# A one-core decoder layer: normalization squares summed on VectorE, router and last shared tile on column groups, and the experts' table written in two parts

## The chip, the cores and the metric

The kernel runs on one core of one Trainium2 chip. The metric is the device time of one execution in microseconds (us). Every view of the trace is of one profiled execution.

## The reference, cut to what matters

One decoder layer over 520 rows of 1024 channels (512 prompt rows and 8 sample rows). Three sub-layers, each followed by a layer norm of `ALPHA * x + f(x)`:

```python
def layer_norm(x, g, b):
    mu = jnp.mean(xf, axis=-1, keepdims=True)
    var = jnp.mean(jnp.square(xf - mu), axis=-1, keepdims=True)
    return (xf - mu) * lax.rsqrt(var + LN_EPS) * g + b

def decoder_layer(...):
    mix = jnp.concatenate([y_a, y_b], axis=-1) @ p['w_out']      # RG-LRU group and convolution group
    x = layer_norm(ALPHA * x + mix, ln1_g, ln1_b)
    x = layer_norm(ALPHA * x + cross_attn(x, mem_k, mem_v, w_q, w_o), ln2_g, ln2_b)
    x = layer_norm(ALPHA * x + moe(x, ...), ln3_g, ln3_b)

def moe(x, ...):
    scores = jax.nn.sigmoid(x @ w_router)            # 64 experts
    # the best 4 of 8 groups, the best 8 experts in them; gates = scores / their sum * 2.5
    return swiglu(x, w1_s, w3_s, w2_s) + routed_experts(x, idx, gates, w1_e, w3_e, w2_e)
```

Each expert is a SwiGLU of 1024 to 256 to 1024 channels, with 3 MB of weights.

## The kernel before, in words

The engines' programs are written out by hand, one block for each (`sync` SP, `gpsimd` POOL, `tensor` PE, `scalar` ACT, `vector` DVE), and meet at semaphores. The PSUM memory is four buffers of 128 x 1024, handed out in the order of a list of groups (`GROUPS`): group g waits until group g-4 has been taken out (`open_group`, `emptied`). `wait_full` waits until PE has finished a group, `wait_out` until it was taken out. An fp32 matmul is two records in the trace.

**Start.** SP loads the five tiles of x, then `w_in` in eight slabs. POOL issues five parameter loads, clears `ident`, issues four state loads and completes the identity (L559). PE turns the tiles of x with it (`turn`, L765), then runs the first projection slab by slab (`mm`, L750); after the seventh slab it turns the parameters.

**First norm.** x lies as `xT`, eight chunks of 128 channels x 520 rows. The mean is one group of matmuls against `mean_d` (all 1/1024). DVE subtracts it from the eight chunks (L1781), ACT squares each (L1406) into `sq`, and `norm_var("var1")` sums the eight squares in PSUM with 8 x 2 matmuls of 260 columns, each waiting for its square on `s_sq`. PE has `v1a` ahead of it and `v1b` and the q projection behind it. ACT takes the root, DVE the reciprocal and the scaling, ACT the gain.

**Second norm**, by halves of 260 rows. `half_var("var2a", 0)` stands in PE's order inside the sample attention's output group `os` (8 samples; it comes before the sixth), with the copies of `os`, its transposes and the second half's projection `xb` behind it. `half_var("var2b", 1)` stands between the shared expert's `h3a0` and `h1b0`; then the router follows, `rt0` and `rt1` (8 matmuls of 64 weight columns x 260 moving columns each; `rt1` waits for each chunk's gain, L1498). On DVE, `half_center` (L1903) is followed by `half_scale`, in the second half with `gated("h3a0", 0)` (L1922) between them. ACT takes `h1b0` with a Silu, then both router groups with a Sigmoid (L1525), PE turns the scores (`rtT`) after tile `x20` of x, and DVE starts the choice of the experts (L1954).

**Routing.** DVE computes the choice, PE sorts the experts by load (`key`, `beaten`, `swT`, `sorted`, `order`) and counts each row's place in its expert (`rank`, `count`). From the order DVE writes `table` (L2027 to L2034, all 64 experts and five tiles at once: the gate in three bf16 parts, and the number among the row's choices by a scan, L2032), then the places (L2037, L2039), the largest count (L2041 to L2044) and `s_table`.

**Head of the experts' stage.** PE does `shared_out(0)` (2 x 2 matmuls of 512 columns from the shared expert's hidden values), waits for `s_table`, and then

```python
            a_step(0, 0)
            a_step(1, 1)
            shared_out(1)
            a_step(2, 2)
            shared_out(2)
            a_step(3, 3)
            shared_out(3)
            shared_out(4)
            wait_out(pe, "so4")
            b_step(0, 0, 16)
            c_step(0, 0, 48)
```

`a_step` finds an expert's rows (five bf16 matmuls of 6 columns of a one-hot from DVE, `oh_step` L2059, against `table`). DVE turns the result into indices (`i_step`, L2065 to L2070), POOL gathers the rows (L660), `b_step` turns them, ACT copies (L1550), `c_step` is the up projection, `t_step` and `y_step` turn the hidden values and project down. `shared_sum(t)` (L2054) on DVE adds shared tile t to `base`. Tile 4 has 8 rows. Of each eight experts five are heavy (112 rows in the first eight, 96 later) and three are light (64 rows). A light expert's up projection (`up_few`) alternates between output partitions 0 to 63 and 64 to 127.

**Experts.** 64 of them in a software pipeline. The weights have four slots; SP issues expert e+4 when `y_step(e)` is done (L495 to L497). Each gather is issued by POOL some steps ahead. At the end the rows written by the experts are loaded again, summed and normalized.

## Time and profile before

| | us |
|---|---|
| median of 3 runs | 1221.01 |
| lowest and highest | 1220.01, 1221.20 |
| the profiled execution's own time | 1218.57 |
| its span, first to last instruction | 1216.8 |
| PE busy in the span | 1138.4 (94%) |
| DVE busy | 411.7 (34%) |
| ACT busy | 257.2 (21%) |
| POOL busy | 176.1 (14%) |

The busy share of PE says which engine most of the time is spent behind, not that each matmul is needed where it stands. The chain of waits names what released each piece. A timeline row gives start and length in us, the engine and line, the operation with its shape, the count that was merged, and in brackets the idle time before it with what ended it. The mean granted TensorE clock of the span is 0.978 of 2.4 GHz.

### The profile page before, as it was taken

How to read it: one execution, taken by the hardware profiler on the slowest of the kernel's cores; microseconds unless marked ns; L12 is line 12 of the kernel's file. 1: busy time of each engine (PE TensorE's matmuls, PEld its weight loads, DVE VectorE, ACT ScalarE, POOL GpSimd, SP SyncE). 2: the span in 40 equal slices, each digit the busy share in tenths (PEclk: the TensorE clock that was granted, in tenths of full speed). 3: DMA queues.
4: the chain of work that ended last, by engine and by line, in shares of the span. 5: the costliest groups of instructions: out<-in, count | busy, mean ns of one | idle time of the engine just before them, and what ended most of it. 6: DMA issues, size and time to landing. Idle time of an engine off the chain costs nothing.

```text
span 1216.8 us, 21054 instructions
## 1 busy us (share of the span) xinstructions
PE 1138.4 (94%) x8302; PEld 759.3 (62%) x8302; DVE 411.7 (34%) x1016; ACT 257.2 (21%) x564; POOL 176.1 (14%) x210
## 2 busy tenths in 40 slices
PE   7999997999988999889999999999999999999964
PEld 6888645877865788657755555555655555655410
DVE  0369997122048324821121212122121121111133
ACT  1101334022041125101122222122222222222200
POOL 3120050000000000111122222122221222212100
PEclk9999998999999999999999999999999999999978
DMA  9630404034047353346999999999999999999496
GB/s 332 235 139 1 156 13 173 1 138 156 1 140 258 157 209 156 155 143 243 352 384 384 385 389 384 380 386 388 388 388 380 371 381 393 384 389 385 161 367 269
DMA packets 66313, 319.16 MB, mean 262 GB/s; under 512 B 10311, under 2 KB 16671, under 8 KB 39629
## 3 DMA queue, kind: packets, MB, share of 16 engines
q1 hardware_dynamic: 51269, 278.60, 59.9%
q0 software_dynamic: 13568, 35.48, 8.6%
q10 hardware_dynamic: 1424, 4.35, 0.9%
q8 instruction: 37, 0.61, 0.2%
q14 instruction: 15, 0.12, 0.0%
HBM read 300.15 MB, written 29.36 MB: 271 GB/s over the span
## 4 chain that ended last, share of the span: by engine, by line
PE 72%; DVE 14%; DMA 10%; issue 1%; ACT 1%; SPq 1%; POOL 0%; POOLq 0%; DVEq 0%
PE psum L750 65%; DVE act_mem L1704 7%; PE psum L765 7%; DMA arena<-in_w_e_dram 5%; DMA arena<-y_rows 3%; DVE mk_mem L1863 2%; DMA arena<-in_w_in_dram 1%; DMA act_mem<-x_rows,idx_x 1%; SPq L541 0%; DVE act_mem L1801 0%; DVE act_mem L1718 0%; DVE rstd L1792 0%; DVE act_mem L1799 0%; DVE act_mem L1769 0%; DMA y_rows<-act_mem,idx_y 0%
## 5 line engine op out<-in xcount | busy, mean ns | idle before, releaser
L750 PE MATMUL psum<-arena,act_mem 128*32 128x128 f32 (+6 forms) x4800 | 512.3, 363 | 6.0 <-DMA arena<-in_w_e_dram 5.1
L750 PEld LDWEIGHTS psum<-arena,act_mem 128*32 128x32 f32 (+5 forms) x4800 | 263.4, 124 | 193.8 <-issue 110.7
L750 PE MATMUL psum<-act_mem,arena 128*128 128x260 f32 (+1 forms) x1728 | 352.4, 366 | 6.0 <-ACT act_mem L1550 2.0
L750 PEld LDWEIGHTS psum<-act_mem,arena 128*128 128x128 f32 x1728 | 306.0, 192 | 49.7 <-ACT act_mem L1550 2.4
L765 PE MATMUL psum<-ident,act_mem 96*128 96x96 f32 (+8 forms) x484 | 76.8, 288 | 19.3 <-POOL ident L559 6.8
L673 POOL DMA_INDIRECT y_rows<-act_mem,idx_y x40 | 45.1, 1128 | 320.2 <-DVE idx_x L2080 170.5
L2092 DVE TENSOR_SCALAR act_mem<-psum,act_mem 96x512 f32<-96x512 f32 (+1 forms) x40 | 29.9, 748 | 155.6 <-PE psum L750 155.6
L1704 DVE SCALAR_TENSOR_TENSOR act_mem<-act_mem,wcb 128x511 f32<-128x511 f32 (+29 forms) x120 | 77.7, 728 | 0.0
L765 PEld LDWEIGHTS psum<-ident,act_mem 96*128 96x128 f32 (+8 forms) x484 | 56.5, 174 | 32.3 <-issue 8.6
L2089 DVE TENSOR_TENSOR act_mem<-act_mem,psum 128x192 f32<-128x192 f32 x35 | 12.4, 354 | 175.5 <-ACT act_mem L1560 175.5
L750 PEld LDWEIGHTS psum<-act_mem 128*96 128x96 bf16 (+4 forms) x371 | 28.5, 126 | 57.2 <-issue 51.2
L1560 ACT ACTIVATE act_mem<-psum 128x192 f32<-128x192 f32 x35 | 11.6, 330 | 189.1 <-PE psum L750 189.1
L1574 ACT ACTIVATE act_mem<-psum,act_mem 96x512 f32<-96x512 f32 (+1 forms) x40 | 27.3, 683 | 111.3 <-PE psum L750 111.3
L666 POOL DMA_INDIRECT y_rows<-act_mem,idx_y x24 | 24.3, 1012 | 162.2 <-DVE idx_x L2070 152.2
L750 PE MATMUL psum<-act_mem 128*96 (+7 forms) x371 | 42.8, 234 | 4.9 <-DVE act_mem L2059 4.9
L765 PEld LDWEIGHTS psum<-ident,mk_mem 64*128 64x128 f32 (+7 forms) x316 | 36.7, 190 | 15.7 <-issue 13.0
L765 PE MATMUL psum<-ident,mk_mem 64*128 64x64 f32 (+7 forms) x316 | 42.4, 276 | 4.3 <-DVE mk_mem L1863 2.6
L750 PE MATMUL psum<-arena,sum_rows 128*32 128x512 f32 (+1 forms) x132 | 23.5, 761 | 21.0 <-DMA arena<-y_rows 21.0
L750 PE MATMUL psum<-arena,kv_mem 128*128 128x512 f32 x96 | 41.8, 593 | 1.2 <-ACT kv_mem L1378 1.2
L1555 ACT ACTIVATE act_mem<-psum 128x384 f32<-128x384 f32 x70 | 30.5, 488 | 24.8 <-PE psum L765 24.8
L660 POOL DMA_INDIRECT act_mem<-x_rows,idx_x x32 | 31.2, 976 | 18.8 <-issue 9.5
L1352 ACT ACTIVATE act_mem<-psum,par 128x520 f32<-128x520 f32 x24 | 16.1, 695 | 81.8 <-PE psum L750 81.7
(264 smaller groups left out, 729.2 us busy)
## 6 DMA issues: line engine op xcount, KB each, us to landing
arena<-in_w_e_dram SPq DMA_DIRECT2D x192, 1024.0 KB
arena<-y_rows SPq DMA_DIRECT2D x8, 2048.0 KB, 23.5
arena<-in_w_in_dram SPq DMA_DIRECT2D x16, 512.0 KB, 18.3
arena<-in_cache_mem_k_dram SPq DMA_DIRECT2D x8, 1024.0 KB, 9.0
arena<-in_cache_mem_v_dram SPq DMA_DIRECT2D x8, 1024.0 KB, 11.8
arena<-in_w_v_dram SPq DMA_DIRECT2D x1, 4096.0 KB, 24.5
arena<-in_w_k_dram SPq DMA_DIRECT2D x1, 4096.0 KB, 13.9
arena<-in_w_out_dram SPq DMA_DIRECT2D x1, 4096.0 KB, 13.9
```

Of the source, the lines that this page charges most:

```text
L660: gp.indirect_dma_start(out=xg[b][0:cap, :], out_offset=None, in_=x2_rows[:, :], in_offset=bass.IndirectOffsetOnAxis(ap=idx_x[0:cap, n:n + ...
L666: gp.indirect_dma_start(out=y_rows[:, :].rearrange("r (h n) -> (r h) n", h=2), out_offset=bass.IndirectOffsetOnAxis(ap=idx_y[:, n:n + 1], ...
L673: gp.indirect_dma_start(out=y_rows[:, :], out_offset=bass.IndirectOffsetOnAxis(ap=idx_y[0:cap, n:n + 1], axis=0), in_=ys[0:cap, b, :], in_ ...
L750: return pe.matmul(out, lhsT, rhs, start=first, stop=last)
L765: return pe.transpose(out, in_, ident[0:n, 0:n])
L1352: act.activation(out, two(bank(name)), func, **kw).then_inc(s_emA, 1)
L1555: last = act.activation(xgT[:, b, 4 * h:4 * h + 4, 0:MCAP], psum[:, 1, 512 * h:512 * h + 4 * MCAP].rearrange("p (k s) -> p k s", k=4), ACT ...
L1574: return act.activation(ys[0:cap, b, 0:512], psum[0:cap, 0, 0:512], ACT.Copy, scale=picked[0:cap, n, 1:2])
L1704: return dve.scalar_tensor_tensor(out, in0, w, in1, ALU.mult, ALU.add)
L1863: ins = dve.tensor_tensor_reduce(junk, kc[:, m, XD * h:XD * h + XD], q_all[:, b, XD * h:XD * h + XD], 1.0, 0.0, ALU.mult, ALU.add, ss[:, m ...
L2089: return dve.tensor_tensor(silu[:, b, 0:192], silu[:, b, 0:192], psum[:, 2, 512 * b + 192:512 * b + 384], ALU.mult)
L2092: return dve.tensor_scalar(ys[0:cap, b, 512:1024], psum[0:cap, 0, 512:1024], picked[0:cap, n, 1:2], None, ALU.mult)
```

## The change

1. **Identity first.** On POOL the clearing of `ident` and its completion stand ahead of the parameter and state loads.
2. **var1.** DVE adds the squares in four pairs (`s_pair`), and PE sums four of them, 4 x 2 matmuls in place of 8 x 2.
3. **var2a, var2b.** DVE adds all eight squares of a half into `xsum` (seven additions, each waiting for the one before, `s_sqsum`), and PE does one matmul of 260 columns in place of eight. In the second half these additions stand ahead of `gated("h3a0", 0)`.
4. **Router.** Each matmul of 260 columns becomes two of 130, to output partitions 0 to 63 and 64 to 127; ACT takes each half with a Sigmoid of its own.
5. **Shared tile 4.** Four column groups of 32 partitions with 256 columns each, 16 records on PE in place of 8 of 512 columns; DVE adds it in four instructions.
6. **Table in two parts.** Columns of the first four experts first, then the places and `oh_step(0)`, `oh_step(1)`; the count after these; the other 60 experts' columns between the shared sums, and `s_table` after them. The subtraction of 1 from the places is gone (POOL numbers the slots from 1). PE no longer waits for `s_table`; its waits for PSUM are put before each user, and `b_step(0)` waits for `so2`, `c_step(0)` for `so3`.

```diff
@@ POOL
+            gp.memset(ident[:, :], 0.0).then_inc(s_const, 1)
+            gp.wait_ge(s_const, 1)
+            gp.affine_select(out=ident[:, :], ...).then_inc(s_const, 1)
             load_parameters(gp, PAR_SPEC[8:], s_par2)
-            gp.memset(ident[:, :], 0.0).then_inc(s_const, 1)
             gp.dma_start(st_h, I["state_rglru_h"][0]).then_inc(s_state, 16)
...
-            gp.wait_ge(s_const, 1)
-            gp.affine_select(out=ident[:, :], ...).then_inc(s_const, 1)
@@ PE
-            norm_var("var1", mean_d, sq, KC)
+            wide("var1", lambda k: mean_d[:, :], lambda k: sq[:, k, :], range(0, KC, 2),
+                 before=lambda k: pe.wait_ge(s_pair, k // 2 + 1))
+            norm_at[0] += KC
...
             def half_var(name, h):
-                half_wide(name, lambda k: mean_d[:, :], lambda k: sq[:, k, :], range(KC), h,
-                          before=lambda k: pe.wait_ge(s_sq, norm_at[0] + k + 1))
-                norm_at[0] += KC
+                pe.wait_ge(s_sqsum, h + 1)
+                half_wide(name, lambda k: mean_d[:, :], lambda k: xsum[:, 0, :], range(1), h)
...
-                    last = mm(ps[0:E, 0:HALF], wr[:, k, :], xT[:, k, HALF * h:HALF * h + HALF], k == 0, k == KC - 1)
+                    for q in range(2):
+                        at = HALF * h + QUARTER * q
+                        last = mm(ps[E * q:E * q + E, 0:QUARTER], wr[:, k, :], xT[:, k, at:at + QUARTER], k == 0, k == KC - 1)
...
+                            for q in (2 * n, 2 * n + 1):
+                                last = mm(ps[32 * q:32 * q + w, 0:256], shT[:, k, t * P:t * P + w],
+                                          w2s[:, k, 256 * q:256 * q + 256], k == 0, k == 1)
...
+            wait_out(pe, "order")
             shared_out(0)
-            pe.wait_ge(s_table, 1)
-            wait_out(pe, "count")
-            wait_out(pe, "x24")
...
+            wait_out(pe, "x24")
             a_step(0, 0)
             a_step(1, 1)
+            wait_out(pe, "rank")
             shared_out(1)
             a_step(2, 2)
+            wait_out(pe, "count")
             shared_out(2)
             a_step(3, 3)
+            wait_out(pe, "so0")
             shared_out(3)
+            wait_out(pe, "so1")
             shared_out(4)
-            wait_out(pe, "so4")
+            wait_out(pe, "so2")
             b_step(0, 0, 16)
+            wait_out(pe, "so3")
             c_step(0, 0, 48)
             b_step(1, 1, 16)
+            wait_out(pe, "so4")
@@ DVE
+            for k in range(0, KC, 2):
+                dve.wait_ge(s_sq, RC + k + 2)
+                dve.tensor_tensor(sq[:, k, :], sq[:, k, :], sq[:, k + 1, :], ALU.add).then_inc(s_pair, 1)
             norm_scale("var1", xT, KC)
...
+            def half_square_sum(h):
+                at = RC + KC + KC * h
+                dve.wait_ge(s_sq, at + 2)
+                total = half(xsum[:, 0, :], h)
+                ins = dve.tensor_tensor(total, half(sq[:, 0, :], h), half(sq[:, 1, :], h), ALU.add)
+                for k in range(2, KC):
+                    link(ins)
+                    dve.wait_ge(s_sq, at + k + 1)
+                    ins = dve.tensor_tensor(total, total, half(sq[:, k, :], h), ALU.add)
+                ins.then_inc(s_sqsum, 1)
...
             half_center("mean2b", 1)
+            half_square_sum(1)
             gated("h3a0", 0)
...
+            def shares(at):
+                sh, tab = share_p[:, :, at], table[:, :, at]
+                link(dve.tensor_copy(tab[:, :, :, 3], sh))
+                link(dve.tensor_tensor(sh, sh, tab[:, :, :, 3], ALU.subtract))
+                link(dve.tensor_copy(tab[:, :, :, 4], sh))
+                link(dve.tensor_tensor(tab[:, :, :, 5], sh, tab[:, :, :, 4], ALU.subtract))
+
+            def turns(last, at):
+                for t in range(TT):
+                    n = chain(dve.tensor_tensor_scan(left[:, t, 0:last], wsum[:, 0:last], sel_p[:, t, 0:last], 0.0,
+                                                     ALU.mult, ALU.add))
+                dve.wait_ge(s_v, n)
+                link(dve.tensor_scalar(table[:, :, at, 2], left[:, :, at], 1.0, None, ALU.subtract))
+
+            shares(slice(0, FIRST))
+            turns(FIRST, slice(0, FIRST))
             wait_full(dve, "rank")
...
             oh_step(0, 0)
             oh_step(1, 1)
+            wait_full(dve, "count")
+            link(dve.tensor_tensor(counts, bank("count")[:, 0:E], bump, ALU.add))
+            dve.tensor_reduce(cmax, counts, AX.X, ALU.max).then_inc(s_emV, 1)
+            wait_out(dve, "count")
+            dve.tensor_copy(over[:, :], cmax).then_inc(s_over, 1)
             i_step(0, 0, None)
             oh_step(2, 2)
             i_step(1, 1, None)
             oh_step(3, 3)
             shared_sum(0)
+            shares(slice(FIRST, E))
             shared_sum(1)
+            turns(E, slice(FIRST, E))
+            dve.sem_inc(s_table, 1)
             i_step(2, 2, None)
             oh_step(4, 4)
             shared_sum(2)
```

## Rows read from the trace of the kernel before

**Rows 1.** The page's chain that ended last, by engine.

```profile
PE 72%; DVE 14%; DMA 10%; issue 1%; ACT 1%; SPq 1%; POOL 0%; POOLq 0%; DVEq 0%
```

**Rows 2.** Timeline of PE, 0 to 36 us.

```profile
6.85 5.92 PE L765 MATMUL psum<-ident,act_mem 128*128 128x128 f32 x40 [6.85 <-POOL ident L559]
...
22.53 10.79 PE L750 MATMUL psum<-act_mem,arena 128*128 128x260 f32 x48 [0.59 <-DMA arena<-in_w_in_dram]
```

**Rows 3.** Timeline of all engines, 255 to 365 us: the first norm.

```profile
263.16 4.94 DVE L1781 TENSOR_TENSOR act_mem<-act_mem,psum 128x520 f32<-128x520 f32 x8 [1.25 <-PE psum L750]
...
269.82 7.18 PE L750 MATMUL psum<-act_mem,mean_d 128*128 128x260 f32 x32
```

**Rows 4.** Timeline of all engines, 385 to 478 us: the second norm, first half.

```profile
413.55 0.43 DVE L1893 TENSOR_TENSOR act_mem<-act_mem 128x260 f32<-128x260 f32 x1
...
414.78 2.77 DVE L1903 TENSOR_TENSOR act_mem<-act_mem,psum 128x260 f32<-128x260 f32 x8 [0.80 <-PE psum L750]
...
419.10 3.77 PE L750 MATMUL psum<-act_mem,mean_d 128*128 128x260 f32 x16
```

**Rows 5.** The same timeline: the second half and the router.

```profile
460.55 2.77 DVE L1903 TENSOR_TENSOR act_mem<-act_mem,psum 128x260 f32<-128x260 f32 x8 [2.98 <-PE psum L750]
...
463.86 3.67 PE L750 MATMUL psum<-act_mem,mean_d 128*128 128x260 f32 x16
...
467.56 0.48 ACT L1493 ACTIVATE rstd<-psum,eps_t 128x260 f32<-128x260 f32 x1 [2.43 <-PE psum L750]
...
470.96 7.23 PE L750 MATMUL psum<-act_mem,gate_w 128*64 128x260 f32 x32
```

**Rows 6.** Timeline of all engines, 478 to 590 us and just before: the scores.

```profile
477.44 0.38 ACT L1525 ACTIVATE kv_mem<-psum 64x260 f32<-64x260 f32 x1
...
478.23 0.38 ACT L1525 ACTIVATE kv_mem<-psum 64x260 f32<-64x260 f32 x1 [0.41 <-PE psum L750]
...
479.14 0.51 PE L765 MATMUL psum<-ident,kv_mem 64*128 64x64 f32 x5
```

**Rows 7.** Timeline of PE, 535 to 600 us: a light expert's up projection.

```profile
557.02 3.85 PE L750 MATMUL psum<-arena,act_mem 128*64 128x256 f32 x32
```

**Rows 8.** Timeline of all engines, 478 to 590 us: DVE's work for the table and the first experts.

```profile
505.00 1.86 DVE L2027 CAST act_mem<-kv_mem 128x320 bf16<-128x320 f32 x1
...
510.59 0.70 DVE L2034 TENSOR_SCALAR act_mem<-kv_mem 128x320 bf16<-128x320 f32 x1
...
512.72 1.40 DVE L2059 TENSOR_TENSOR act_mem<-act_mem,gate_w 128x560 bf16<-128x560 f32 x2
...
514.24 0.16 DVE L2065 TENSOR_REDUCE act_mem<-psum 112x2 f32<-112x6 f32 x1
...
516.53 1.21 DVE L2054 SCALAR_TENSOR_TENSOR act_mem<-act_mem,psum 128x1024 f32<-128x1024 f32 x1
```

**Rows 9.** The same timeline and its continuation: PE in that stretch.

```profile
505.00 3.67 PE L750 MATMUL psum<-act_mem 128*128 128x512 f32 x8
...
513.61 17.71 PE L750 MATMUL psum<-act_mem 128*112 128x6 bf16 x52 [4.93 <-DVE act_mem L2059]
...
534.77 7.79 PE L750 MATMUL psum<-act_mem,arena 128*128 128x112 f32 x64 [1.01 <-ACT act_mem L1550]
```

**Rows 10.** The chain of waits: a gather from issue to landing.

```profile
676.75 10.88 DMA act_mem<-x_rows,idx_x
```

**Rows 11.** Windows: us, busy of PE, PEld, DVE, ACT, POOL, granted clock, DMA share, GB/s.

```profile
388.50:391.20 2.70, 0.14 (x2) 0.10 (x2) 2.49 (x13) 0.00 (x0) 0.00 (x0) 1.00 1.08 405
...
512.00:518.80 6.80, 5.19 (x15) 2.86 (x16) 5.41 (x15) 0.00 (x0) 2.83 (x3) 0.50 1.01 427
...
771.30:774.80 3.50, 3.50 (x20) 2.00 (x18) 0.00 (x0) 0.00 (x0) 0.94 (x1) 0.51 1.00 414
...
822.00:860.00 38.00, 38.00 (x368) 22.12 (x366) 8.12 (x24) 8.47 (x23) 10.21 (x10) 1.00 1.02 385
```

**Rows 12.** Timeline of PE, 766 to 776 us: a wait for an expert's weights.

```profile
770.76 5.44 PE L750 MATMUL psum<-arena,act_mem 128*64 128x256 f32 x32 [2.33 <-DMA arena<-in_w_e_dram]
```

More of the change, by code:

```diff
@@ L2025, in _ @@
             dve.sem_inc(s_order, 1)
-            link(dve.tensor_copy(table[:, :, :, 3], share_p))
-            link(dve.tensor_tensor(share_p, share_p, table[:, :, :, 3], ALU.subtract))
-            link(dve.tensor_copy(table[:, :, :, 4], share_p))
-            link(dve.tensor_tensor(table[:, :, :, 5], share_p, table[:, :, :, 4], ALU.subtract))
-            for t in range(TT):
-                n = chain(dve.tensor_tensor_scan(left[:, t, :], wsum, sel_p[:, t, :], 0.0, ALU.mult, ALU.add))
-            dve.wait_ge(s_v, n)
```

57 lines of the change are left out of this document (30 added, 27 removed).

## The prediction

> **What bounds the kernel now.** I read the page's chain first: 72% of it is TensorE, 14% VectorE [rows 1]. A microsecond taken off a matmul counts only where TensorE itself is late, so each stretch that the change touches has to be read in the timeline, for what starts the instruction behind it. Four patterns come out. At the start a weight slab ends the last wait before the dense work: TensorE waited 0.59 us for it and ran on at 22.53 [rows 2]. At the first norm TensorE runs without a pause through the variance, and the q projection stands behind it [rows 3]. In the second half of the second norm ScalarE is as late as TensorE: the first Sigmoid follows its predecessors on ScalarE, the second waited for TensorE by 0.41 us only [rows 6]. From the expert order to the first expert VectorE is late: TensorE waited 4.93 us for the first one-hots [rows 9]. In the experts' stage TensorE is busy 38.00 of 38 us and the DMA share is 1.02 [rows 11]: two limits at once, and each expert's weights are issued only when TensorE frees a slot, so a stage that begins earlier takes its stream of weights along.
>
> **Identity first: 0.** TensorE began at 6.85, released by the identity [rows 2]. Whatever it gains there it waits longer for the slab before 22.53. The parameter loads go out behind a clear, a wait and the completion, so at most about 1 us later on POOL's queue; they are wanted when the seventh slab is done, at about 33 us [rows 2]. I keep 0.3 either way, as the slabs share the DMA engines with these loads.
>
> **var1: -3.6.** 32 records took 7.18, 0.224 each [rows 3]; 16 of them go, 3.6. The pair sums come behind the centre, which ends at 263.16 + 4.94 = 268.10. One costs between the centre's own pace, 4.94 / 8 = 0.62, and twice the half-width addition, 0.86 [rows 3, 4]. So the first is ready by 269.0 at the latest, where TensorE wants it at 269.82, and the fourth by 271.5, wanted after 12 records at 272.5. The additions cost nothing, since VectorE would otherwise wait for the root; without that cover they would cost 2.5 to 3.4. Root, reciprocal, scaling and gain move as one, so the q projection starts 3.6 earlier and everything behind it moves.
>
> **var2a: -1.4.** The centre ends at 414.78 + 2.77 = 417.55 [rows 4]. Seven additions follow, each waiting for the one before. One lies between 0.35 (the pace of the centre, where nothing waits) and 0.50; I take 0.43 from its row plus 0.03 for the hand-over, an estimate, 3.2 in all: 420.8. TensorE arrives at 419.10, waits 1.7 with the last three samples, their copies, the transposes and xb queued behind it, then needs one matmul, some 0.6 with the restart: 421.4 in place of 422.87 [rows 4]. 1.4 less for all of these; by the bounds 1.1 to 2.2. VectorE's reciprocal and scaling come earlier too and are hidden by xb.
>
> By a rule of the Trainium skill (VectorE: DVE Perf Modes, "The DRAIN you can't avoid") a semaphore after each operation costs nothing extra. By it the seven additions would take the lower bound, 2.4, and this term would be 2.2 and the next 1.0. No row here shows these additions, so I stay with the row of the addition that did wait, 0.43 against the centre's 0.35 [rows 4].
>
> **var2b: -0.2.** The centre ends at 463.32, the additions at 466.5. TensorE is done with h3a0 at about 464.0 and now waits 2.6 us, with h1b0 and the router queued behind. With 0.7 for the restarted matmul the root starts at about 467.3, in place of 467.56 [rows 5]. The saved 3.67 us of matmuls turn into a wait for VectorE. `gated` for h3a0 comes 3.2 later, and nobody near wants it.
>
> **Router: -0.6.** Alternating output halves do run beside each other: 32 records of 64 weight columns and 256 moving ones took 3.85 in a light expert, 0.120 each, against 0.224 for 260 columns on the whole array [rows 7, 3]. So the 7.23 us of both groups [rows 5] become some 3.9, ready before 475. But ScalarE comes to the first Sigmoid only at 477.44 - 0.2 = 477.2. Four half-width Sigmoids cost between 0.19 and 0.38 each; I take 0.28: done at 478.3 in place of 478.61. TensorE turned tile x20 first and began the scores at 479.14 [rows 6]; now x20 is turned long before, and it begins at 478.4. With var2b that is 0.8 less (bounds 0.4 and 1.1), where 3.3 us of matmuls were removed. From there TensorE's shared groups and the routing chain move as one.
>
> **The head of the experts' stage: -9.2.** VectorE took from 505.00 to 510.59 + 0.70 = 511.29 for the table, ten instructions [rows 8]. For four experts the same ten are all small; with 0.16 as for the smallest row and a hand-over they cost 1.8, and with the places (0.5) VectorE is at 507.3. Two one-hots, 1.40: 508.7. TensorE ends shared tile 0 at 505.00 + 3.67 = 508.67 [rows 9] and goes straight on, where it waited until 513.61. Then on VectorE: count 0.7, two index steps 0.55 each, two one-hots 0.7 each, shared sum 1.2 (513.1); the other 60 experts' columns, 60/64 of 6.3 = 5.9, around a second sum 1.2 (520.2); index step, one-hot, sum (522.7), and the same again (525.3) [rows 8]. TensorE meanwhile has three tiles of 3.5, four finds of 0.35 and tile 4, which falls from 3.5 to 0.9 if four column groups run together: 521.5. `b_step(0)` waits for the third sum, 522.7; with 1.1 for the turns and 1.0 for the copy its rows are ready at 524.9, and `c_step(0)` waits for the fourth sum: 525.4 to 525.6 in place of 534.77 [rows 9]. 9.2 less. VectorE is late next. Bounds: with VectorE quicker TensorE's own 523.7, 11.1; with VectorE 1.5 slower, 7.7. The gather of expert 0 goes out near 510.8; at the 10.88 us of a slow one [rows 10] it lands at 521.7, a microsecond before it is wanted. POOL's wait for `s_table` (520.2) puts gathers 2 and 3 about where they were relative to the kernel's start, and they are wanted after `c_step(1)`, some 17 us later. Weights 2 and 3 are still released by the order.
>
> **TensorE's clock: +1.7.** It was at half from 512.0 to 518.8, behind the 4.93 us of idleness [rows 9, 11]; that fall goes and is within the 9.2. But the change makes new gaps: 1.7 (var2a), 2.6 (var2b), about 2.5 before the scores, and 1.2 and 1.3 with only transposes between around `b_step(0)`. The clock was at half behind a wait of 2.33 [rows 12, 11], and at full behind a stretch with 0.14 busy in 2.70 [rows 11]. So gaps of this size may do it or not. At half clock for 3.5 us dense work loses 1.7. I count one such loss; a fall at var2b is hidden, as the router has 2 us to spare.
>
> The Trainium skill (TensorE: Matmul & The Clock Gate, "HAM oscillation") warns that idle waits between bursts of matmuls bring the half clock back; that speaks against the sums on VectorE, and this trace agrees (0.51 in 771.3 to 774.8).
>
> **Sum.** -3.6 - 1.4 - 0.8 - 9.2 + 1.7 = -13.3. The profiled execution took 1218.57, so 1205.3 for it. It is 2.4 below the median of the three runs, 1221.01; against the median, which is what will be compared, 1207.7.
>
> **Rivals.**
> - *The clock falls at no gap, or at three.* 1206.0 and 1211.1. For it: rows on both sides.
> - *Weights come late more or less often.* A wait of 2.33 and 3.5 us at half clock cost 4.1 [rows 11, 12]; the pattern occurs twice. The DMA share of 1.02 says that little is needed to make one or lose one. One or two more: 1211.8 or 1215.9. One or two fewer: 1203.6 or 1199.5. Against it: issue and use both move with TensorE.
> - *The head gives less*: the gather behind the weights of experts 2 and 3, or VectorE slower on strided slices. 1.5 to 3 less gain, 1209 to 1211.
> - *Column groups don't run together in the router.* It ends near 478, and its 0.6 is gone; tile 4 keeps 3.5, but VectorE is later anyway. 1208.3.
> - *Slower than before.* In the experts' stage the weights become late in each of the eight rounds of eight experts, as TensorE meets the full queues in another phase: 8 x 4.1 less the two there are, +24.6, so 1232. It decides from four more such waits on (16.4 against 13.3). Nothing but the share of 1.02 speaks for it.
>
> **Chances.** Forecast with none to two losses of clock, 1206 to 1209.5: 0.55. Three, or a smaller gain at the head: 0.15. More late weights: 0.11. Fewer: 0.14. About as before, if three or so late weights come in: 0.03. Slower: 0.02. The range 1202.0 to 1214.5 leaves out most of the two fewer and the two more. About 0.2%, 2.4 us, is what a measurement of this kernel can tell from no change; faster by more than that is 0.95.
>
> **What would show it.** Right: q projection 3.6 earlier; in the waits, TensorE waiting for VectorE's additions by 1.7 and 2.6; the scores only 0.8 us earlier than the shift before them, although the router takes 4; no wait of 4.9 for one-hots, and `c_step(0)` released by the fourth shared sum. Wrong: if `c_step(0)` waits for the gather; if the clock's record shows half in new places with dense work in them; if the waits for weights have another count, for then the stream and not the head decides the end.

## The result, and the profile after

| | us |
|---|---|
| after, median of 4 runs | 1210.40 (1204.30 to 1210.91) |
| before beside it, 4 runs | 1221.11 (1220.01 to 1222.46) |
| ratio | 0.9902, 95% interval 0.9879 to 0.9924 |
| profiled execution of after | 1210.91 (span 1209.1); before 1218.57 (1216.8) |

10.7 us faster; forecast were 1207.7 in a range of 1202.0 to 1214.5. The two profiled executions are 7.7 us apart, where the sum had 13.3, and what follows compares these.

The page's chain by engine, answering to [rows 1]:

```profile
PE 67%; DVE 16%; DMA 13%; ACT 2%; issue 1%; SPq 1%; DVEq 0%; POOLq 0%
```

TensorE's share of the chain fell by 5 points and that of VectorE and the transfers rose: work was taken off TensorE and waits stand in its place. The timeline of PE shows each. A row gives start, length, form, count, and in brackets the idle time before it and what ended it:

```profile
4.82 6.81 PE L770 MATMUL psum<-ident,act_mem 128*128 128x128 f32 x40 [4.82 <-DMA act_mem<-in_x_prompt_dram]
...
22.53 7.72 PE L755 MATMUL psum<-act_mem,arena 128*128 128x260 f32 x34 [0.51 <-DMA arena<-in_w_in_dram]
...
262.03 1.12 PE L755 MATMUL psum<-act_mem,mean_d 128*128 128x260 f32 x4 [1.64 <-DVE act_mem L1831]
...
387.64 0.38 PE L770 MATMUL psum<-ident,mk_mem 128*32 128x128 f32 x2 [2.28 <-DVE mk_mem L1879]
...
412.23 0.71 PE L755 MATMUL psum<-act_mem,mean_d 128*128 128x260 f32 x2 [1.05 <-DVE act_mem L1909]
419.16 0.71 PE L755 MATMUL psum<-act_mem,mean_d 128*128 128x260 f32 x2 [1.78 <-DVE act_mem L1935]
...
465.41 0.71 PE L755 MATMUL psum<-act_mem,mean_d 128*128 128x260 f32 x2 [2.72 <-DVE act_mem L1935]
...
469.56 3.95 PE L755 MATMUL psum<-act_mem,gate_w 128*64 128x130 f32 x64
...
477.22 0.52 PE L770 MATMUL psum<-ident,kv_mem 64*128 64x64 f32 x5 [2.69 <-ACT kv_mem L1537]
477.67 3.60 PE L770 MATMUL psum<-ident,act_mem 128*128 128x128 f32 x16
...
508.96 0.39 PE L755 MATMUL psum<-act_mem 128*112 128x6 bf16 x5 [0.57 <-DVE act_mem L2095]
509.52 12.34 PE L755 MATMUL psum<-act_mem 128*112 128x6 bf16 x55 [0.17 <-DVE act_mem L2095]
522.35 1.14 PE L770 MATMUL psum<-ident,act_mem 112*128 112x112 f32 x8 [0.49 <-DVE act_mem L2084]
524.67 9.32 PE L755 MATMUL psum<-act_mem,arena 128*128 128x112 f32 x64 [1.17 <-DVE act_mem L2084]
...
762.26 5.81 PE L755 MATMUL psum<-arena,act_mem 128*64 128x256 f32 x96 [2.44 <-DMA arena<-in_w_e_dram]
```

The start gained 2.0 and had lost it by 22.53, which is to the hundredth where TensorE ran on in [rows 2]. The variance matmuls of the second norm are one group of two, behind waits of 1.78 and 2.72 for the last addition (L1935). The router takes 3.95 in place of 7.23 [rows 5], and behind it stands a new wait of 2.69. The wait of 4.93 for the one-hots [rows 9] is down to 0.57, and the first expert's up projection starts at 524.67 in place of 534.77, released by the fourth shared sum (L2084).

Two rows are longer than their like in other executions: 3.60 for 16 transposes (1.97 elsewhere) and 9.32 for the up projection (7.79 in [rows 9]). The windows say why (us, busy of PE, PEld, DVE, ACT, POOL, granted clock, DMA share, GB/s):

```profile
389.10:392.50 3.40, 3.40 (x10) 2.66 (x9) 0.86 (x4) 0.56 (x2) 0.00 (x0) 0.53 1.02 424
426.60:430.00 3.40, 3.40 (x10) 2.63 (x9) 0.00 (x0) 3.38 (x7) 0.00 (x0) 0.52 1.08 356
477.80:481.20 3.40, 3.40 (x17) 3.40 (x18) 1.67 (x19) 1.92 (x4) 0.00 (x0) 0.52 0.38 154
525.60:529.00 3.40, 3.40 (x19) 3.40 (x18) 0.60 (x2) 0.00 (x0) 0.00 (x0) 0.52 1.03 313
```

Four stretches of dense matmuls at half clock, 1.2 of 2.4 GHz, each behind a short idle time of TensorE, and none of them in the profile of before. Below, such a stretch is called a fall. In a table of steps, each from one row of the timeline to another, the account closes. "Root" is ScalarE's square root of the second half, "order" is VectorE's cast of the expert order; the stretch from the score transposes to mean2a differs only by one of the falls and has no row of its own:

| step (profiled executions) | before | after | gained |
|---|---|---|---|
| start of the first mean matmuls | 262.00 | 262.03 | 0.0 |
| from there to the attention's score transposes | 129.13 | 125.61 | 3.5 |
| from mean2a to mean2b, 1.7 of a clock fall taken off | 45.88 | 44.7 | 1.2 |
| mean2b to the second half's root | 7.65 | 7.57 | 0.1 |
| root to order, 1.6 of a clock fall taken off | 37.08 | 36.6 | 0.5 |
| order to the first up projection | 30.13 | 20.31 | 9.8 |
| the four clock falls | | | -6.6 |
| **to the second expert's up projection** | 544.44 | 535.91 | **8.5** |

The 9.8 of the head hold the fall of before that went: from 512.0 to 518.8 its clock was at 0.50 over 5.19 us of work [rows 11], so about 2.6 of the 9.8 are clock, an estimate.

The experts' stage passes this on whole: its end moves from 1151.27 to 1142.80, again 8.5. Waits for an expert's weights hold TensorE 7.9 us in after and 5.1 in before, but before lost another 3.4 to two falls there, the one at 771.3 [rows 11] and this one, and after none:

```profile
925.00:928.40 3.40, 3.40 (x18) 1.89 (x20) 0.00 (x0) 0.00 (x0) 1.23 (x2) 0.50 1.02 424
```

The tail gives back 0.8.

### The profile page after: what moved, and what is told of

Read it like the earlier page. It is cut to its first block, busy times and chain, and to the rows that moved or that the text cites. A ratio compares the mean times of both kernels' runs of the same rounds, so it can differ in the third digit from the quotient of the medians.

```text
span 1209.1 us, 21090 instructions
## 1 busy us (share of the span) xinstructions
PE 1124.7 (93%) x8298; PEld 751.8 (62%) x8298; DVE 421.4 (35%) x1046; ACT 258.0 (21%) x566; POOL 176.2 (15%) x210
## 4 chain that ended last, share of the span: by engine, by line
PE 67%; DVE 16%; DMA 13%; ACT 2%; issue 1%; SPq 1%; DVEq 0%; POOLq 0%
PE psum L755 60%; DMA arena<-in_w_e_dram 8%; DVE act_mem L1717 7%; PE psum L770 6%; DMA arena<-y_rows 3%; DVE mk_mem L1879 2%; DMA arena<-in_w_in_dram 1%; SPq L546 1%; DVE act_mem L1935 0%; ACT act_mem L1500 0%; DVE act_mem L2084 0%; DVE act_mem L1814 0%; ACT act_mem L1509 0%; DVE act_mem L1731 0%; DVE act_mem L2095 0%
## 5 line engine op out<-in xcount | busy, mean ns | idle before, releaser
L755 PEld LDWEIGHTS psum<-arena,act_mem 128*32 128x32 f32 (+5 forms) x4800 | 260.6, 123 | 196.7 <-issue 107.5
L755 PE MATMUL psum<-act_mem,arena 128*128 128x260 f32 (+1 forms) x1728 | 357.7, 369 | 7.1 <-DMA arena<-in_w_o_dram 1.3
L755 PEld LDWEIGHTS psum<-act_mem,arena 128*128 128x128 f32 x1728 | 309.7, 195 | 52.6 <-DMA arena<-in_w_in_dram 2.4
L770 PE MATMUL psum<-ident,act_mem 96*128 96x96 f32 (+8 forms) x484 | 79.5, 296 | 16.5 <-DVE act_mem L1818 6.8
L770 PEld LDWEIGHTS psum<-ident,act_mem 96*128 96x128 f32 (+8 forms) x484 | 59.1, 178 | 28.7 <-issue 12.3
L755 PE MATMUL psum<-act_mem 128*96 (+7 forms) x379 | 37.8, 226 | 0.8 <-DVE act_mem L2095 0.7
## 6 DMA issues: line engine op xcount, KB each, us to landing
arena<-in_w_in_dram SPq DMA_DIRECT2D x16, 512.0 KB, 18.1
```

The lines of the kernel that those rows point to most:

```text
L755: return pe.matmul(out, lhsT, rhs, start=first, stop=last)
L770: return pe.transpose(out, in_, ident[0:n, 0:n])
```

## The experiments

Two kernels are compared by their ratios to the runs of before beside them, whose medians were 1221.15, 1221.66, 1221.97 and 1220.49 in the four comparisons. Single executions of one kernel spread over 2 to 8 us, more than most of the parts are worth, so a part is read from its step in the trace, and the times say only whether the step reached the end.

### The same kernel again: after_again

The kernel after without an edit.


> The changed kernel once more, unaltered. Theory A (the clock's falls move): the stretches repeat to 0.2 us, but the half-clock pieces of 3.4 us lie at other gaps than in the first profile (389, 427, 478 and 526 us), each worth 1.7 us where dense matmuls are in it; single times spread over some 6 us, from 1204 to 1211, and the mean granted clock goes with them. Rival B (the falls belong to the places): the same four pieces within 1 us of the same times, and times within 0.3% of each other.

Measured: 1208.95 (1207.71 to 1209.85), ratio 0.9897 (0.9882 to 0.9911). Every step between falls repeats to 0.1 us (order to first up projection 20.24, released as before), but two of the four falls have moved:

```profile
525.60:529.00 3.40, 3.14 (x26) 3.15 (x27) 1.77 (x5) 0.04 (x1) 0.42 (x1) 1.00 1.02 381
477.80:481.20 3.40, 2.22 (x22) 1.82 (x20) 0.00 (x0) 3.23 (x6) 0.00 (x0) 1.00 0.00 0
469.80:473.20 3.40, 3.40 (x10) 2.68 (x9) 3.37 (x7) 1.35 (x3) 0.00 (x0) 0.51 0.00 0
22.70:26.10 3.40, 3.40 (x10) 2.60 (x9) 0.00 (x0) 0.00 (x0) 0.00 (x0) 0.52 1.03 412
```

None at the first up projection, though the wait before it is 1.17 in both executions, and none at the scores; one in front of the router, one at the start and one at a wait for weights. The other two stay at their gaps: the clock is at 0.56 from 391.6 to 395.0 and at 0.52 from 428.9 to 432.3, each the same piece of work as in after. So theory A holds for two of the four falls and rival B for the other two, and the times spread over 2.1 us, as rival B had it, and not over 6.

The fall in front of the router shows how one can be hidden. Timeline of PE:

```profile
468.32 0.71 PE L755 MATMUL psum<-act_mem,mean_d 128*128 128x260 f32 x2 [2.71 <-DVE act_mem L1935]
468.86 5.36 PE L755 MATMUL psum<-act_mem,arena 128*128 128x260 f32 x16
...
480.12 0.51 PE L770 MATMUL psum<-ident,kv_mem 64*128 64x64 f32 x5 [1.18 <-ACT kv_mem L1537]
```

The wait of 2.71 is that of after (2.72), where the clock stayed at 1.00. Here it fell, the next 16 records took 5.36 in place of 3.67, and the wait before the scores shrank from 2.69 to 1.18.

### The table alone: table_only

Norms and router as before; the two-part table, the last shared tile and the early identity stay.

```diff
-            wide("var1", ..., lambda k: sq[:, k, :], range(0, KC, 2), before=...)
+            norm_var("var1", mean_d, sq, KC)
...
-                    for q in range(2):
-                        at = HALF * h + QUARTER * q
-                        last = mm(ps[E * q:E * q + E, 0:QUARTER], ...)
+                    last = mm(ps[0:E, 0:HALF], ...)
```

with the second norm's edit of the next experiment as well.

> The kernel before with the identity, the table in two parts and tile 4 on column groups only; var1, var2a, var2b and the router as before. Theory A: the head of the experts' stage comes 9.8 us earlier (c_step(0) at 525 where it was at 534.8) less at most one fall of 1.7, so 8 to 10 us less than before: 1211 to 1213. Rival C (the stream of weights sets the end): waits for weights take back most of it, 3 us or less gained, 1218.

Measured: 1211.81 (1208.89 to 1215.73), ratio 0.9928 (0.9910 to 0.9945). The step from the order to the first up projection is 20.25, that of after. So the head's 9.8 stand by themselves in the step; by the ratio the kernel gains 8.8 (6.7 to 11.0), as theory A had it.

### The second norm as before: no_half_sums

```diff
-            half_square_sum(0)
...
-            half_square_sum(1)
...
-                pe.wait_ge(s_sqsum, h + 1)
-                half_wide(name, ..., lambda k: xsum[:, 0, :], range(1), h)
+                half_wide(name, ..., lambda k: sq[:, k, :], range(KC), h, before=...)
```

> The changed kernel with the squares of both halves summed on TensorE again (var2a, var2b as before). Theory A: var2a takes 1.2 us longer and var2b 0.3, but the gaps of 1.8 and 2.7 us go, and with them one fall of the clock of 1.7 in xb or at the router in most runs: 0 to 1 us faster than the changed kernel, or the same. Rival D (the sums on VectorE are worth their 1.5 and cause no fall): 1.5 slower than the changed kernel.

Measured: **1245.78** (1234.07 to 1252.76), ratio 1.0187 (1.0148 to 1.0226). No theory had this. The norm and the head read as they should (order to up projection 20.31); at the scores the wait is again 2.69, and behind it the clock is at half for 6.8 us, so that root to order takes 39.54. The loss is in the experts' loop, which runs a round of eight experts a turn. Timeline of PE:

```profile
781.24 0.69 PE L770 MATMUL psum<-ident,act_mem 128*128 128x128 f32 x2 [5.33 <-issue]
865.21 0.69 PE L770 MATMUL psum<-ident,act_mem 128*128 128x128 f32 x2 [6.19 <-issue]
949.79 0.68 PE L770 MATMUL psum<-ident,act_mem 128*128 128x128 f32 x2 [6.40 <-issue]
1034.90 0.68 PE L770 MATMUL psum<-ident,act_mem 128*128 128x128 f32 x2 [6.12 <-issue]
```

Once a turn TensorE stands still for 5.3 to 6.4 us, released by nothing that the profile shows ("issue"), and then loses more at half clock. One queue of the page has changed (packets, MB, share), first this kernel, then after:

```profile
q8 instruction: 73, 1.20, 0.4%
```

```profile
q8 instruction: 37, 0.61, 0.2%
```

I read it as the fetching of TensorE's program, 16 KB a packet. In after, as in before, no packet of it lies between 700 and 1075 us: the loop is run from what is held. Here each of four turns fetches nine packets, two of them inside each stop. What the edit did, beyond the norm, is to put 14 more f32 matmuls in front of the loop, so that the loop lies elsewhere in the program.

### The place of the loop by itself: waits_in_front

All of the kernel after, with 128 more waits for a semaphore that is satisfied already (built as 64 instructions), where TensorE waits for x.

```diff
-            pe.wait_ge(s_const, 2)
+            for _ in range(129):
+                pe.wait_ge(s_const, 2)
```

> The kernel after with 64 instructions more in TensorE's program and no other work: waits for the constants' semaphore that is satisfied already, placed where TensorE waits for x at the start. This asks why the kernel without the half sums took 1245.8. Theory P (placement): what that kernel changed was not the second norm alone but the place of the experts' loop in TensorE's program; its 14 more f32 matmuls push the loop by some tens of instructions, the loop then no longer stays in the sequencer's memory, and each of its rounds fetches its instructions anew (73 packets on the instruction queue instead of 37, a stop of 5.3 to 6.4 us with cause 'issue' in every round, each followed by a stretch at half clock). Then this kernel, whose norms, scores and head are those of the kernel after, takes 1240 to 1250 us and shows about 73 packets. Theory N (the norm): the missing half sums themselves bring the stops, by what they leave late. Then this kernel stays at 1207 to 1213 us with 37 packets. Price of the waits alone: TensorE's start, 4.8 us, later by up to 2 us, which the identity's part has shown to cost 0.

Measured: **1247.35** (1245.55 to 1250.58), ratio 1.0207 (1.0183 to 1.0230). Theory P, shown: instructions that do nothing, in a stretch where they delay nothing that matters (order to up projection 20.29), cost 38 us at the other end of the kernel.

```profile
695.94 0.69 PE L770 MATMUL psum<-ident,act_mem 128*128 128x128 f32 x2 [6.73 <-issue]
...
780.57 0.69 PE L770 MATMUL psum<-ident,act_mem 128*128 128x128 f32 x2 [5.80 <-issue]
```

```profile
q8 instruction: 82, 1.34, 0.5%
```

Five such stops where no_half_sums had four, and so 82 packets and not the 73 of the expectation: 45 more than after, nine a turn again. Five stops (30.4 us), smaller ones behind them (5.5) and the falls make the loss. The Trainium skill (Runtime: NRT & Kernel Launch, "Instruction fetch mechanics") says that an engine's instruction memory is a FIFO refilled in blocks of 16 KiB, for TensorE 128 KiB, and that a taken branch whose target isn't in the current two-page window stalls until the page is fetched. The trace agrees in the size of a packet and in the stall, and adds its length, 5.3 to 6.7 us. It does not agree with two pages for TensorE: in after no packet comes between 700 and 1075, though 77 us of a turn hold 733 matmuls and as many weight loads, more than two of the page's 256-instruction blocks. By the page's 128 KiB eight blocks are held, and the nine packets a turn are one more, an estimate that fits a loop pushed across a boundary; that the runs show only from outside: after, before and the kernel with the table alone (some 24 instructions more than after) are free of it, the kernels with some 56 and with 64 more are not. The 24 and 56 are estimates, at four instructions (two weight loads, two matmuls, as the records show them) for each f32 matmul, and leave the waits out. Where between 24 and 56 the boundary lies was not measured.

### Norm and router as before, the loop in place: no_half_no_cols

The edits of no_half_sums and no_column_groups (below) in one kernel:

```diff
-            half_square_sum(0)
...
-                        last = mm(ps[E * q:E * q + E, 0:QUARTER], ...)
+                    last = mm(ps[0:E, 0:HALF], ...)
```

> The kernel after without the half sums of the second norm and without the router's column groups; the pair sums of var1, the experts' head and the early identity stay. Ahead of the experts' loop TensorE's program is then two f32 matmuls shorter than that of the kernel after, so the loop stands where it stood. Theory P (placement): no stops in the rounds, 37 packets, and a time that the sum gives: 1.4 for var2a and 0.8 for the scores later than the kernel after, 1210.5 to 1213.5. Theory N (the norm): the stops of 5 to 6 us a round come back with the norm of before, 1240 or more. Against the kernel with the table's edit alone (1211.8), which differs in var1 only, this should be 3 us faster if var1 is worth its 3.6, and the same if it is given back.

Measured: 1208.66 (1206.03 to 1213.53), ratio 0.9891 (0.9867 to 0.9915), 37 packets. Theory P again, by the packets and the missing stops; the time is 1.8 below the range that was expected. Against the table alone (0.9928), which differs in var1, var1 is worth 0.0037 of 1221, 4.5 us; the two intervals overlap, so this agrees with the 3.5 of the step and doesn't prove it. Against after there is no difference that can be told, where the steps say 1.8 (1.2 + 0.1 + 0.5): the half sums and column groups do their work, and the waits that they leave (1.78, 2.72, 2.69) may let the clock fall.

Over all profiles, the clock fell right behind the wait of 2.7 at var2b in six of the ten kernels with half sums, and at that place in none of the four without. Before the scores the wait was 2.69 in three profiles (after, no_half_sums, memset_rest_late), and the clock fell behind it each time; where a fall in front of the router had shortened it to 1.2, it did not. The fall at about 427 is no sign of the half sums: it is in every profile but that of before, the kernels without half sums included. Up to the order the clock was at half for 17.0 us here, for 23.8 and 27.3 in the two executions of after.

### Router as before alone: no_column_groups

```diff
-                    for q in range(2):
-                        at = HALF * h + QUARTER * q
-                        last = mm(ps[E * q:E * q + E, 0:QUARTER], wr[:, k, :], xT[:, k, at:at + QUARTER], ...)
+                    last = mm(ps[0:E, 0:HALF], wr[:, k, :], xT[:, k, HALF * h:HALF * h + HALF], ...)
```

> The kernel after with the router of before: each half's scores on the whole array in one group of eight and one sigmoid for each half; the last shared tile stays on column groups. TensorE's program is 16 f32 matmuls shorter ahead of the experts' loop. Theory A (the sum of the prediction): the router's eight matmuls of a half at 260 columns take 7.23 us for both halves instead of 3.95, but most of it lies beside VectorE's and ScalarE's chain to the scores, so that the scores come 0.6 to 1.0 us later, no more: 1210 to 1212.5. Rival (TensorE's time counts in full): 3.3 us later, 1213 to 1214. The router takes 7.2 in the row of TensorE in both. Packets on the instruction queue tell whether the loop's place matters here: 37 if it stays, more and a time above 1235 if it doesn't.

Measured: 1207.61 (1204.74 to 1211.38), ratio 0.9884 (0.9862 to 0.9907), 36 packets; below both expected ranges, and by the intervals not to be told from after. Timeline of PE:

```profile
470.51 7.23 PE L755 MATMUL psum<-act_mem,gate_w 128*64 128x260 f32 x32
477.67 1.09 PE L770 MATMUL psum<-ident,act_mem 128*128 128x128 f32 x8
478.69 0.51 PE L770 MATMUL psum<-ident,kv_mem 64*128 64x64 f32 x5
```

The router takes its 7.23 and TensorE never waits, so theory A holds by the step. From root to order it is 37.08, as before, against 36.56 in after_again: 0.5 lost, not 3.3. What bounds the scores in after is ScalarE, whose timeline has two table loads in that place:

```profile
473.03 1.28 ACT L1515 ACT_TABLE_LOAD   x1
474.32 0.39 ACT L1515 ACTIVATE act_mem<-psum 128x260 f32<-128x260 f32 x1
474.73 1.28 ACT L1536 ACT_TABLE_LOAD   x1
476.02 0.27 ACT L1536 ACTIVATE kv_mem<-psum 64x130 f32<-64x130 f32 x1
```

And where the clock then falls, as in the profiled execution of after (root to order 38.20), column groups lose 1.1.

### Filling the wait before the scores: up_before_scores

```diff
             turn_x(0)
+            shared_up("h3b0", 0)
             wait_out(pe, "rt1")
```

> The kernel after with one group moved: the shared expert's first up projection for tile 0, of about 3.5 us on TensorE, is put ahead of the turning of the scores, and its gate on VectorE with it. In the kernel after TensorE waits 2.69 us for the second half's sigmoid at that place and its clock then falls to 0.52 for 3.4 us. Theory A: the wait is filled by work that was to be done anyway; the wait (2.7) goes, the fall at this place goes too where it stood (1.7), the turning of the scores starts up to 1 us later than it could: the order of the experts comes 1 to 3 us earlier and the kernel takes 1206.5 to 1209.5. Rival (VectorE bounds): what follows the scores on VectorE sets the order, and the scores come later by the matmuls put in front: 1210 to 1212.

Measured: 1207.12 (1203.08 to 1208.38), ratio 0.9870 (0.9849 to 0.9891). The wait is gone, and root to order is 35.47 with a fall at 466.6 inside it. After_again has 36.56 with a fall in the same place, so the gain like for like is 1.1. Without a fall there, after has 38.20 (its clock falls behind the scores instead) and the kernel memset_up_first below, with the same edit, 34.47: 3.7. The time lies in theory A's range. The rival falls: TensorE, not VectorE, was late behind the scores.

### GpSimd's memset out of VectorE's way: memset_late

```diff
+            gp.wait_ge(m_oh, 2)
             for n in range(2):
                 gp.memset(xg[n], 0.0).then_inc(m_z, 1)
```

> The changed kernel with POOL's two clears of the gather buffers held back until the first two one-hots are made. In the changed profile the first cast of the table (20 elements) took 1.35 us and ended with POOL's clears. Theory A (a VectorE instruction waits out POOL's clear): that cast falls to 0.2 to 0.3, the first one-hot comes 1.0 us earlier, and c_step(0) 0.9 to 1.0 earlier relative to the expert order; 1.0 us faster in all if nothing else moves. Rival E (the cast is slow because of its strided output): it stays at 1.3, no difference.

Measured: 1204.66 (1202.26 to 1209.24), ratio 0.9869 (0.9850 to 0.9889). In after, DVE and POOL:

```profile
504.18 1.85 POOL L656 MEMSET act_mem<- 128x1024 f32 x2
```

```profile
504.72 1.35 DVE L2058 CAST act_mem<-kv_mem 128x20 bf16<-128x20 f32 x1
506.11 0.19 DVE L2059 TENSOR_TENSOR kv_mem<-kv_mem,act_mem 128x20 f32<-128x20 f32 x1
506.33 0.20 DVE L2060 CAST act_mem<-kv_mem 128x20 bf16<-128x20 f32 x1
```

and with the memset moved:

```profile
501.69 0.20 DVE L2059 CAST act_mem<-kv_mem 128x20 bf16<-128x20 f32 x1
```

A cast of 20 elements takes 1.35 if GpSimd's memset runs, and ends with it (504.18 + 1.85 = 506.03); the next cast of the same form takes 0.20. Rival E falls. The Trainium skill (SBUF — State Buffer, "SBUF: two separate sides") has VectorE, in a 2-port perf mode, and GpSimd share one pair of ports as an exclusive lock, and whoever comes second waits for the whole instruction. The trace agrees with the lock; no row tells the mode of the cast. Not every operation is held: the memset runs later now, beside VectorE's one-hot, which takes the 0.81 that it takes elsewhere:

```profile
505.34 1.85 POOL L657 MEMSET act_mem<- 128x1024 f32 x2 [4.15 <-DVE act_mem L2096]
```

```profile
506.22 0.81 DVE L2096 TENSOR_TENSOR act_mem<-act_mem,gate_w 128x640 bf16<-128x640 f32 x1
```

Before had the same stop. Its first cast of the table stands in [rows 8] with 1.86 beside a memset, and its like two rows on took 0.70:

```profile
507.54 0.70 DVE L2029 CAST act_mem<-kv_mem 128x320 bf16<-128x320 f32 x1
```

Order to up projection falls from 20.31 to 19.08, 1.2, since VectorE's list bounds that step. The whole kernel gains more than this by its median, 4 us. The rest is not the memset's: in the profiled execution the order, ahead of which nothing was edited, already came at 501.33 in place of 504.36 and 505.62, with the clock at half for 17.2 us up to there in place of 23.8 and 27.3.

### The rest of the table later as well: memset_rest_late

```diff
             shared_sum(4)
+            shares(slice(FIRST, E))
+            turns(E, slice(FIRST, E))
+            dve.sem_inc(s_table, 1)
             c_step(0, 0)
```

> The kernel with GpSimd's memset put behind the first one-hots (1204.7 in its own comparison), and with it the rest of the experts' table (the four share steps over 300 elements, the scan over 64 and the turns, 5.2 us of VectorE) moved behind VectorE's fourth shared sum. Between the order and the first expert's up projection TensorE waits 0.35 and 1.17 us for VectorE's shared sums in the kernel with the memset moved; its own work there (shared sums, places, finds) is about 17.5 us of 19.1. Theory A (TensorE bounds the head now, VectorE only by its waits): the two waits go and no more, the step from the order to the first up projection falls from 19.08 to 17.4 to 18.0, and the kernel takes 1203 to 1205. Rival (VectorE's list still bounds): all 5.2 come off, up to the landing of the first gather, 3 us: 16.1, 1201 to 1203. Third: the rest of the table is then late for the fourth find and the wait comes back behind the first up projection: no gain, 1204.5 to 1206.

Measured: 1206.16 (1203.51 to 1207.83), ratio 0.9862 (0.9838 to 0.9886). 5.2 us of VectorE are moved away and the step goes from 19.08 to 18.55 only: one wait goes, the other is 1.05 still. TensorE's own 17.5 us bound the head now. The step gains less than theory A had (17.4 to 18.0), though it is nearest to it in kind, and the time shows nothing: 0.9862 against the 0.9869 of memset_late is no difference, and 1206.16 is the upper end of the third theory's range.

### Fillers together: memset_up_first and all_three

The first has these two edits:

```diff
+            gp.wait_ge(m_oh, 2)
             for n in range(2):
                 gp.memset(xg[n], 0.0).then_inc(m_z, 1)
...
             turn_x(0)
+            shared_up("h3b0", 0)
```

> The two edits that filled waits, together: GpSimd's memset behind the first one-hots, and the shared expert's up projection ahead of the turning of the scores. Each comes off a different step: 19.1 instead of 20.3 from the order to the first up projection, 35.5 instead of 36.6 from ScalarE's root of the second half to the order. If both hold together the two steps sum to 54.6 (56.8 in an execution of the kernel after without a clock fall in them, 58.5 in the profiled one), and the kernel takes 1203 to 1205.5; if the gains of the stage are given back in waits for weights, 1205 to 1208.

Measured: 1202.58 (1201.00 to 1206.91), ratio 0.9840 (0.9813 to 0.9867). Steps 34.47 and 19.09, together 53.6, 1.0 less than expected; after had 58.5 in its profiled execution and 56.8 in the second. The time is just below the expected range.

The second moves the rest of the table too, `shares(slice(FIRST, E))`, `turns(E, ...)` and the table's semaphore, behind `shared_sum(4)`:

```diff
             shared_sum(4)
+            shares(slice(FIRST, E))
+            turns(E, slice(FIRST, E))
```

> The three edits together (memset behind the first one-hots, the up projection ahead of the scores, the rest of the table behind the fourth shared sum): the steps 35.5 and 17.4 to 18.0, together 53 to 53.5, the kernel 1201.5 to 1204.5 if the experts' stage keeps what it gets, and 1204 to 1207 if the waits for weights in the rounds of eight grow by it, as they did from 5.1 to 7.9 us in the profiled execution of the kernel after.

Measured: **1201.87** (1200.64 to 1203.84), ratio **0.9831** (0.9808 to 0.9854), steps 35.47 and 18.54. The second step misses its range (17.4 to 18.0), the time is in it. This version beats both kernels, by 20 us and by 7 to 8.5; its interval lies below that of after. From the two fillers alone it can't be told (0.9831 against 0.9840).

### The router as before once TensorE no longer waits: three_whole_router

```diff
-                        last = mm(ps[E * q:E * q + E, 0:QUARTER], wr[:, k, :], xT[:, k, at:at + QUARTER], ...)
+                    last = mm(ps[0:E, 0:HALF], wr[:, k, :], xT[:, k, HALF * h:HALF * h + HALF], ...)
```

> The kernel with all three edits (1201.9 in its own comparison), with the router of before: whole array, 7.2 us of TensorE in place of 3.8, one sigmoid a half. In the kernel after the column groups were worth 0.5 us on the step from ScalarE's root to the order (37.08 with the whole router, 36.56 with column groups and no clock fall), because TensorE then waited for ScalarE's table loads and sigmoids. With the up projection put in that wait TensorE has no idle time from the router to the order's matmuls. Theory A: what a saving on TensorE is worth is set by whether TensorE waits behind it. Then the same edit undone here costs 2.5 to 3.4 us: the step reads 37.0 to 38.9 in place of 34.5 to 35.5, and the kernel takes 1203.5 to 1206. Rival (ScalarE and VectorE bound this step anyway): 0 to 1 us, step 35.5 to 36.5, 1201 to 1203.

Measured: 1204.63 (1203.77 to 1206.92), ratio 0.9864 (0.9847 to 0.9880). This kernel, then the one with all three edits and column groups, PE:

```profile
471.36 7.23 PE L756 MATMUL psum<-act_mem,gate_w 128*64 128x260 f32 x32
...
483.05 0.51 PE L771 MATMUL psum<-ident,kv_mem 64*128 64x64 f32 x5
```

```profile
471.19 3.77 PE L756 MATMUL psum<-act_mem,gate_w 128*64 128x130 f32 x64
...
479.42 0.51 PE L771 MATMUL psum<-ident,kv_mem 64*128 64x64 f32 x5
```

From root to order 38.93 against 35.47, both with a fall at about 466: the whole 7.23 - 3.77 = 3.46, theory A's upper end. By the ratios it is 4.0, with intervals that just overlap. The same edit was worth 0.5 where TensorE waited behind it.

## Why the prediction was right, point by point

- **Identity first**, 0: held. 2.0 gained at the start, 0.0 at 22.53.
- **var1**, -3.6: held, 3.5. The four pair sums (268.27 to 270.80) never make TensorE wait.
- **var2a**, -1.4: 1.2. The wait was 1.78 where 1.7 was written. The seven additions took from 415.90 to 419.10, 3.20, the 3.2 of the sum. By the Trainium skill's rule (VectorE: DVE Perf Modes, "The DRAIN you can't avoid") the semaphore after each would have cost nothing and they would have taken 2.4; the trace does not bear that out here: 0.46 for a linked addition against 0.35 for the unlinked centre. The centre reads PSUM and the additions do not, but that hardly matters, as the unlinked pair sums took 2.53 / 4 = 0.63 where the centre of the same width took 4.94 / 8 = 0.62.
- **var2b**, -0.2: 0.1, with a wait of 2.72 against 2.6 written.
- **Router**, -0.6: 0.5. The column groups run together (3.95), four sigmoids took 0.27 or 0.28 each, and the scores began at root + 11.06 in place of root + 11.58.
- **The head**, -9.2: 9.8, inside its bounds of 7.7 and 11.1. The ten small instructions took 1.2 longer at the first cast, for the memset, which no term had; the 60 experts' columns took 5.2, not 5.9. Both go back to one row: the 1.86 in [rows 8] was taken for work, and 1.2 of it was a wait for the memset. The sum's last stretch, 522.7 to 525.3, is also 0.15 longer than its terms. Released by the fourth shared sum, as written.
- **TensorE's clock**, +1.7: the mis-sized term. It counted one fall at half clock in dense work; the profiled execution had four more than before in front of the experts (6.6), and after_again four too, two of them at the same gaps and two at others. The rule to count one was a choice between rows on both sides. What failed is the thought that a gap either lets the clock fall or not: behind the same 2.7 at var2b it fell in six profiles of ten. Why, stays open. A fall at var2b was rightly taken for hidden (after_again has one at 469.9, and its step from root to order is 36.56 all the same); behind the scores, where TensorE runs until 495 without a pause and VectorE waits for it, it counts in full.
- **The rivals on the weights**: waits of 7.9 us where there were 5.1, with no clock falls where there were two; the two differences nearly cancel. The stage neither gave nor took, and that was luck: no term of the sum had either of them.
- **The place of the loop**: in no term and in no rival. By its diff the change takes 22 f32 matmuls out of TensorE's program in front of the loop (8 in var1, 14 in the second norm) and puts 20 in (16 in the router, 4 in tile 4), so the loop hardly moved. With the 14 left in, the kernel is 35 us slower (no_half_sums). That too was luck.

The terms without the clock add up to 15.1 measured and 15.0 forecast. The profiled execution was forecast at 1205.3 and took 1210.91: 4.9 of the 5.6 are the clock's excess (6.6 for 1.7), 0.8 the tail. The median of 1210.40 lies 2.7 above the forecast and outside the 1206 to 1209.5 that had the largest chance, 1208.95 of the second comparison 1.2 above; how much of the median's 2.7 is clock is not settled, since only one execution of each comparison has a trace.

The head and var1 carry the change, var1 by its step alone. Half sums and column groups, 1.8 by the steps, are not seen in any time.

## What to carry to other kernels

- Before matmuls are taken off TensorE, ask who is late behind them. Here a saving of 3.3 to 3.5 us on TensorE was worth 0.5 with ScalarE late and 3.46 once independent matmuls filled the wait. The filler is work that was to be done anyway, and with it the clock fell behind the scores in none of four profiles, where it had fallen in all three that kept the wait of 2.69.
- In a kernel with a loop on TensorE, look at the instruction queue's packets after every edit in front of the loop. If they double, as from 37 to 73 and 82 here, look for stops in the loop before blaming the edit's own work: this kernel lost 3% to 64 instructions that do nothing.
- Where executions spread by 5 us, read a part worth 1 us from a step between two rows that no fall lies in, and not from medians.

## What the runs showed of the hardware that was not expected

- The loop's instructions are fetched anew in each turn, nine packets of 16 KB, if some 56 or 64 instructions more stand in front of it: 5.3 to 6.7 us of idle TensorE a turn, 35 to 38 us in all.
- GpSimd's memset holds up a VectorE cast from f32 to bf16 in SBUF until it ends: 1.35 in place of 0.20 for 20 elements, 1.86 in place of 0.70 for 320. A one-hot of two SBUF inputs beside the same memset takes its usual 0.81.
- The granted clock falls to 0.52 behind an idle time of 2.7 us (at var2b) in six profiles of ten and stays at 1.00 in the others; behind 1.17 in front of the first up projection it fell in after and not in after_again. A fall is worth 1.5 to 1.7 us where the work behind it is dense and wanted, and nothing where a wait behind it absorbs it. How much of the spread of 2 to 8 us between executions of one program comes from this is not shown.
